# A hybrid transformer trunk on one NeuronCore: forget-gate bias as extra rows of a matmul, and one ring of six weight pieces

## The reference, cut to what matters

```
h = rms_norm(x); u = h @ w_in            # 1024 -> 5384 columns
y_pool = pool_mixer(u[pool])             # trailing windows 2, 4, 8, 16
y_conv = conv_module(u[conv])            # GLU, depthwise conv of 31 taps, LayerNorm, swish
y_attn = forgetting_attention(q, k, v, f_logit)
x = x + (sum of gate_i * (y_i @ w_br_i)) @ w_out
```

## Time and profile before

| | |
|---|---|
| median of 3 runs | 1668.14 us (1666.18 to 1669.09) |
| the profiled execution | 1673.39 us |
| its span, first to last instruction | 1671.5 us |
| mean granted TensorE clock in it | 0.989 of full speed |
| busy share of the span | PE 98%, DVE 77%, ACT 63%, POOL 4% |
| HBM read | 450.74 MB |

### The profile page before, as it was taken

How to read it: one execution, slowest core, us unless ns; L and a number is a source line. 1 busy time by engine, 2 the same in 40 slices (tenths; PEclk the granted TensorE clock), 3 DMA queues, 4 the chain that set the end, 5 groups by cost and what they waited for, 6 DMA issues and landing times.

```text
span 1671.5 us, 25101 instructions
## 1 busy us (share of the span) xinstructions
PE 1634.1 (98%) x9644; PEld 1433.8 (86%) x9644; DVE 1290.0 (77%) x1097; ACT 1056.3 (63%) x908; POOL 61.9 (4%) x60
## 2 busy tenths in 40 slices
PE   7999989999899998999999999999999999999998
PEld 7998989999898897888888888888888888888887
DVE  5973764444697476897997998997988987987986
ACT  5444444454554454677777777777777777777775
POOL 0121100000012110000000000000000000000000
PEclk9999999999999998999999999999999999999999
DMA  9543455556454343799999999999999999999993
GB/s 335 167 146 106 127 167 171 191 175 200 126 170 133 103 133 120 258 377 369 327 374 354 344 371 340 358 372 334 365 371 333 363 375 334 359 377 334 359 377 132
DMA packets 231294, 452.48 MB, mean 271 GB/s; under 512 B 6992, under 2 KB 80720, under 8 KB 231120
## 3 DMA queue, kind: packets, MB, share of 16 engines
q1 hardware_dynamic: 231248, 451.82, 76.7%
HBM read 450.74 MB, written 1.05 MB: 270 GB/s over the span
## 4 chain that ended last, share of the span: by engine, by line
PE 93%; DVE 4%; ACT 2%; issue 1%; DMA 0%; ACTq 0%; DVEq 0%
PE bank L278 28%; PE bank L280 27%; PE bank L279 27%; PE bank L1292 2%; PE bank L1308 1%; DVE w_low L268 1%; PE bank L1326 1%; ACT w_high L264 1%; PE bank L1041 1%; PE bank L1129 1%; DVE h_full L628 1%; DVE rinv L618 0%; PE bank L1131 0%; PE bank L1148 0%; PE bank L1092 0%
## 5 line engine op out<-in xcount | busy, mean ns | idle before, releaser
L268 DVE TENSOR_TENSOR w_low<-raw,w_high 128x2048 fp32r<-128x2048 f32 x427 | 977.8, 2291 | 284.4 <-ACT w_high L264 283.2
L264 ACT ACTIVATE w_high<-raw 128x2048 fp32r<-128x2048 f32 x427 | 818.9, 1919 | 378.1 <-PE bank L280 376.7
L278 PE MATMUL bank<-w_high,hg_high 128*128 128x512 f32 x896 | 354.5, 396 | 0.7 <-issue 0.7
L280 PE MATMUL bank<-w_high,hg_low 128*128 128x512 f32 x896 | 350.1, 391 | 0.0
L279 PE MATMUL bank<-w_low,hg_high 128*128 128x512 f32 x896 | 349.3, 390 | 0.0
L278 PE MATMUL bank<-h_high,w_high 128*128 128x256 f32 x1056 | 301.8, 286 | 6.4 <-DVE h_low L623 4.8
L280 PE MATMUL bank<-h_high,w_low 128*128 128x256 f32 x1056 | 295.3, 280 | 0.0
L279 PE MATMUL bank<-h_low,w_high 128*128 128x256 f32 x1056 | 295.3, 280 | 0.0
L278 PEld LDWEIGHTS bank<-h_high,w_high 128*128 128x128 f32 x1056 | 200.8, 190 | 11.8 <-issue 9.4
L279 PEld LDWEIGHTS bank<-h_low,w_high 128*128 128x128 f32 x1056 | 199.1, 189 | 1.6 <-issue 1.4
L280 PEld LDWEIGHTS bank<-w_high,hg_low 128*128 128x128 f32 x896 | 168.6, 188 | 36.0
(11 more groups left out here) (242 smaller groups left out, 1586.6 us busy)
## 6 DMA issues: line engine op xcount, KB each, us to landing
raw<-exp_w SPq DMA_DIRECT2D x336, 1024.0 KB, 5.3
raw<-w_in SPq DMA_DIRECT2D x42, 1024.0 KB, 5.1
raw<-ffn_w SPq DMA_DIRECT2D x33, 1024.0 KB, 5.3
raw<-w_out SPq DMA_DIRECT2D x8, 1024.0 KB, 4.9
raw<-w_br_attn SPq DMA_DIRECT2D x4, 1024.0 KB, 5.0
raw<-w_br_pool SPq DMA_DIRECT2D x2, 1024.0 KB, 5.2
raw<-w_br_conv SPq DMA_DIRECT2D x2, 1024.0 KB, 4.9
cst<-consts SPq DMA_DIRECT2D x1, 1280.0 KB, 13.4
```

The lines of the kernel that those rows point to most:

```text
L264: nc.scalar.activation(wh[c % SPLIT][:], raw[c % RAW][:], ACT.Copy).then_inc(s["high_done"], 1)
L268: nc.vector.tensor_tensor(wl[c % SPLIT][:], raw[c % RAW][:], wh[c % SPLIT][:].bitcast(F32), ALU.subtract).then_inc(s["split_done"], 1)
L278: pe.matmul(dst, lh, rh, start=start and i == 0, stop=False)
L280: last = pe.matmul(dst, ll, rh, start=False, stop=stop and i == len(terms) - 1)
```

## The change

**Ring.** `raw`, `wh` and `wl` are six buffers each. `raw` and `wl` share their memory: the low half of a piece is written over the loaded piece. So the load of piece c now waits until PE has used piece c-6 (not until its low half is made), and `split_high` waits only for the load, no longer for PE.

**Bias rows.** GpSimd no longer makes `decay`. DVE writes the negated `lf` of the 8 heads twice into a zeroed tile `nlf` (columns 0 to 7 and 32 to 39). After piece 8 PE forms its running sums with three float32 matmuls into bank 6 (`bias_sums`): 64 rows x 384 columns. ACT rounds them to fp32r rows `crow` (step 11), DVE replaces the rows of the second copy by what the rounding lost (step 11). `head_scores` starts with one fp32r matmul over all 384 columns whose weights pick head h's two rows (`sel8`, one column read 128 times), then adds the mask in fp32r twice, then q.k. The rest of the `c_i` term is left to the softmax, where it drops out.

**Order of VectorE.** `head_norm(h)` stands in step 14+h, behind `head_max(h)`; a few taps (`TAPS_AHEAD`) stand between, and `TAPS_AT` is less for steps 12 to 15. The sum stays 62.

The core of the diff:

```diff
-TAPS_AT = {..., 10: 8, 11: 8, 12: 8, 13: 8, 14: 7, 15: 7}
+TAPS_AT = {..., 10: 8, 11: 8, 12: 6, 13: 5, 14: 5, 15: 4}
+TAPS_AHEAD = {12: 2, 13: 3, 14: 2, 15: 3}
...
-        raw = [sb(f"raw{i}", [P, PIECE]) for i in range(RAW)]
-        wh = [sb(f"w_high{i}", [P, PIECE], F32R) for i in range(SPLIT)]
-        wl = [sb(f"w_low{i}", [P, PIECE], F32R) for i in range(SPLIT)]
+        with ExitStack() as loaded:
+            raw = [loaded.enter_context(nc.sbuf_tensor(f"raw{i}", [P, PIECE], F32)) for i in range(RING)]
+        wl = [sb(f"w_low{i}", [P, PIECE], F32R) for i in range(RING)]
+        wh = [sb(f"w_high{i}", [P, PIECE], F32R) for i in range(RING)]
...
         def load_piece(sp, c, r, src, k):
-            if not (isinstance(r, int) and c < RAW):
-                sp.wait_ge(s["split_done"], num(c - RAW + 1, r))
+            if not (isinstance(r, int) and c < RING):
+                sp.wait_ge(s["used"], num(c - RING + 1, r))
...
         def split_high(act, c, r=0):
-            if not (isinstance(r, int) and c < SPLIT):
-                act.wait_ge(s["used"], num(c - SPLIT + 1, r))
...
# GpSimd
-                for h in range(HEADS):
-                    if h >= 2:
-                        pool.wait_ge(s["scores"], 8 * l + h - 1)
-                    for k, (m, tile) in enumerate(((C_UPTO, 0), (C_UPTO, 1), (C_ONES, 0))):
-                        nc.gpsimd.tensor_scalar(decay[:, h % 2, k, :], C(m), lf[:, tile, h:h + 1], None,
-                                                ALU.mult).then_inc(s["decays"], 1)
+                pool.wait_ge(s["f_soft"], 2 * l + 2)
+                nc.gpsimd.memset(nlf[:], 0.0).then_inc(s["nlf_zero"], 1)
+                pool.wait_ge(s["nlf_zero"], l + 1)
+                nc.gpsimd.memset(crow[64:P, :].bitcast(F32), 0.0).then_inc(s["rows_zero"], 1)
...
# ScalarE
+                    if n == 5:
+                        nc.scalar.activation(identr[:], ident, ACT.Copy).then_inc(s["consts_r"], 1)
+                        nc.scalar.activation(maskr[:], C(C_MASK), ACT.Copy).then_inc(s["consts_r"], 1)
+                    if n == 11:
+                        act.wait_ge(s["bias_sum"], l + 1)
+                        nc.scalar.activation(crow[0:64, :], bank[6][0:64, 0:384], ACT.Copy).then_inc(s["bias_high"], 1)
...
# VectorE
-                    if 15 <= n <= 22:
-                        head_norm(n - 15)
                     if 14 <= n <= 21:
                         head_max(n - 14)
+                    run_taps(TAPS_AHEAD.get(n, 0))
...
+                    if 14 <= n <= 21:
+                        head_norm(n - 14)
...
+                    if n == 11:
+                        dve.wait_ge(s["bias_high"], l + 1)
+                        nc.vector.tensor_tensor(crow[32:64, :], bank[6][32:64, 0:384], crow[32:64, :].bitcast(F32),
+                                                ALU.subtract).then_inc(s["bias_low"], 1)
...
# TensorE
+                def bias_sums():
+                    pe.wait_ge(s["nlf_in"], 2 * l + 2)
+                    pe.wait_ge(s["qk_root"], 4 * l + 3)
+                    pe.matmul(bank[6][0:64, 0:128], nlf[:, 0, :], C(C_UPTO), start=True, stop=True)
+                    pe.matmul(bank[6][0:64, 128:384], nlf[:, 0, :], C(C_UPTO, 2), start=True, stop=False)
+                    pe.matmul(bank[6][0:64, 256:384], nlf[:, 1, :], C(C_UPTO), start=False,
+                              stop=True).then_inc(s["bias_sum"], 1)
...
-                    pe.matmul(B[:, 0:128], q[:, 0:P], k[:, 0:P], start=True, stop=False)
-                    pe.matmul(B[:, 0:128], decay[:, h % 2, 0, :], C(C_AFTER), start=False, stop=False)
-                    pe.matmul(B[:, 0:128], ident, C(C_MASK), start=False, stop=True)
-                    pe.matmul(B[:, 128:384], q[:, P:S], k, start=True, stop=False)
-                    pe.matmul(B[:, 128:256], decay[:, h % 2, 2, :], C(C_AFTER), start=False, stop=False)
-                    pe.matmul(B[:, 128:384], decay[:, h % 2, 1, :], C(C_ONES, 2), start=False, stop=False)
-                    pe.matmul(B[:, 256:384], ident, C(C_MASK), start=False, stop=True).then_inc(s["scores"], 1)
+                    pe.matmul(B[:, 0:384], sel8[:, h:h + 1].to_broadcast([P, P]), crow[:], start=True, stop=False)
+                    pe.matmul(B[:, 0:128], identr[:], maskr[:], start=False, stop=False)
+                    pe.matmul(B[:, 256:384], identr[:], maskr[:], start=False, stop=False)
+                    pe.matmul(B[:, 0:128], q[:, 0:P], k[:, 0:P], start=False, stop=False)
+                    pe.matmul(B[:, 128:384], q[:, P:S], k, start=False, stop=True).then_inc(s["scores"], 1)
```

More of the change, by code:

```diff
@@ L49 @@
 NEG = -1e30
-RAW = 6
-SPLIT = 3
+RING = 6
 PIECE = 2048
@@ L159, in trunk @@
             vt = mb("vt", [P, TT, 512])
-            decay = mb("decay", [P, 2, 3, P])
+            crow = mb("bias_rows", [P, 3 * P], F32R)
+            maskr = mb("mask_r", [P, P], F32R)
+            identr = mb("ident_r", [P, P], F32R)
+            nlf = mb("neg_log_forget", [P, TT, 64])
+            sel8 = mb("head_rows", [P, 8], F32R)
             prob = mb("prob", [P, 2, 384])
@@ L209, in trunk @@
             squares norm_stats norm_root norm_h h_high_done h_low_done norm_step
-            f_logits f_soft decay_in decays unit_part ln_taps unit_used_act unit_used_dve
+            f_logits f_soft nlf_zero rows_zero nlf_in consts_r head_rows bias_sum bias_high bias_low unit_part ln_taps unit_used_act unit_used_dve
             qk_sq qk_stats qk_root pool_in_ready pooled_ready pool_lin
@@ L220, in trunk @@
         x_in = [sem(f"x_in{m}") for m in range(4)]
-        raw_in = [sem(f"raw_in{i}") for i in range(RAW)]
+        raw_in = [sem(f"raw_in{i}") for i in range(RING)]
         def C(i, n=1):
@@ L235, in num @@
         def num(c, r):
-            return c if isinstance(r, int) and r == 0 else r * RAW + c
+            return c if isinstance(r, int) and r == 0 else r * RING + c
         def unit_ready(eng, l, u):
@@ L272, in take_piece @@
             pe.wait_ge(s["split_done"], num(c + 1, r))
-            return fold(wh[c % SPLIT][:], k), fold(wl[c % SPLIT][:], k)
+            return fold(wh[c % RING][:], k), fold(wl[c % RING][:], k)
         def products(pe, dst, terms, start=True, stop=True):
@@ L560, in job @@
                     if not isinstance(j, int):
-                        for k in range(SPLIT):
+                        for k in range(3):
                             split_high(act, c + k, r0)
@@ L573, in job @@
                         t_high(r + 1)
-                        silu(r * RAW + (MOE0 + 6))
+                        silu(r * RING + (MOE0 + 6))
                         split_high(act, c + 9, r)
@@ L807, in mixer @@
                         dve.wait_ge(s["act_step"], 2 * l + 2)
-                        nc.vector.tensor_tensor(fg[:, 5, :], fg[:, 4, :], fg[:, 3, :],
-                                                ALU.subtract).then_inc(s["decay_in"], 1)
+                        dve.wait_ge(s["nlf_zero"], l + 1)
+                        for at in (0, 32):
+                            nc.vector.tensor_tensor(nlf[:, :, at:at + 8], fg[:, 3, :].rearrange("p (t h) -> p t h", t=TT),
+                                                    fg[:, 4, :].rearrange("p (t h) -> p t h", t=TT),
+                                                    ALU.subtract).then_inc(s["nlf_in"], 1)
+                        nc.vector.tensor_tensor(sel8[:], ident[:, 0:8], ident[:, 32:40],
+                                                ALU.add).then_inc(s["head_rows"], 1)
+                    if n == 11:
+                        dve.wait_ge(s["bias_high"], l + 1)
+                        nc.vector.tensor_tensor(crow[32:64, :], bank[6][32:64, 0:384], crow[32:64, :].bitcast(F32),
+                                                ALU.subtract).then_inc(s["bias_low"], 1)
                     run_taps(TAPS_AT.get(n, 0))
@@ L976, in job @@
                     r0, c = j * EXP_BLOCKS, MOE0
-                    for k in range(SPLIT if isinstance(j, int) else 0, 4):
+                    for k in range(3 if isinstance(j, int) else 0, 4):
                         split_low(dve, c + k, r0)
@@ L996, in middle @@
                         split_low(dve, c + 9, r)
-                        mult(r + 2, r * RAW + (MOE0 + 8))
+                        mult(r + 2, r * RING + (MOE0 + 8))
                         split_low(dve, c + 10, r)
@@ L1116, in ln_sum @@
                     ins.then_inc(s[name], 1)
-                def head_scores(h):
-                    pe.wait_ge(s["decays"], 3 * (8 * l + h) + 3)
+                def bias_sums():
[5 more added lines that the diff above has]
+                              stop=True).then_inc(s["bias_sum"], 1)
+                def head_scores(h):
+                    if h == 0:
+                        pe.wait_ge(s["bias_low"], l + 1)
+                        pe.wait_ge(s["consts_r"], 2 * l + 2)
+                        pe.wait_ge(s["head_rows"], l + 1)
```

(3 more changed lines are left out.)

12 lines of the change are left out of this document (5 added, 7 removed).

## The result

The changed kernel takes 1642.77 us (median of 4 runs, 1642.18 to 1649.69), the kernel before 1667.99 us (1666.18 to 1669.09). The ratio is 0.986, with a 95% interval of 0.9845 to 0.9874: 25.2 us faster, where 18.9 were forecast and the range of 1637 to 1661 holds the time. The ratios are formed from fast executions alone; two slow ones of the kernel before (2315.08 and 2743.64 us, at a mean granted clock of 0.659 and 0.554) are left out of them.

A forecast was written before the change was run, and what follows sets the result against it. PE was taken to bound the kernel, with 93% of the chain of waits. The terms -18.4 + 2.4 + 0 - 2.9 + 0 gave -18.9 us, from 1673.4 to 1654.5 and, at the median, 1649 us; range 1637 to 1661.

The forecast's parts named there:

- The scores: Attention on PE: each head's scores fall from 2.77 to 1.62 us, 18.4 us gained over 16 heads; bounds 13.6 to 20.8.
- The bias sums: After piece 8 on PE: three added float32 matmuls cost 1.2 us a layer, 2.4 us for both; bounds 1.6 and 3.0.
- The order of VectorE: Attention on DVE: `head_norm(h)` one step earlier and the moved taps cost zero.
- half of the gain is lost: Rival: DVE or ACT late in the faster attention, or late expert pieces; PE saves 9 us net, 1659 us; chance 0.12.
- PE stands three pieces behind DVE there: Attention, step 14: the argument given against the rival that DVE's work there loses half of the gain.
- PE needs the result two pieces later (over 14 us): Attention: the reason given that `head_norm` one step earlier, with DVE waiting for ACT's exponentials, costs zero.
- The ring: Last part of each mixer: idle times of 0.92 and 0.51 us go, 2.9 us for both layers; bounds 0 and 4.0.
- which the change doesn't touch: Last part of a mixer: of PE's 7.2 us idle, the rest beyond 0.92 and 0.51 us is the normalisation, unchanged.
- The expert jobs: Expert jobs: later loads from the ring cost nothing, jobs still 123.6 us; bounds 0 and 17 us.
- 4.1 us of reserve: Expert jobs: 16.3 us from load issue to end of use, 12.2 needed, 4.1 left for queueing on ACT and DVE.
- The pace: Rival: another start shifts the dense stage to PE's faster pace, winning 7 to 8 us more, 1640 us; chance 0.13.
- the offset of 5.3 us to the median: The profiled execution, 1673.4 us, lay 5.3 us above the runs' median of 1668.1, lowering the forecast from 1654.5 to 1649.2.

The follow-up runs named there:

- qk_apart: The changed kernel with the first q.k product moved up between the bias matmul and the masks, same five matmul lines: 1648.27 us, ratio 0.9888.
- order_only: The kernel before with only VectorE's new order (`TAPS_AT`, `TAPS_AHEAD`, place of `head_norm`): 1667.53 us, ratio 1.0005.
- order_undone: The changed kernel with VectorE's old order, the division one step later and all taps after the split: 1649.42 us, ratio 0.99.
- bias_only: The kernel before with the bias rows and new scores alone, old buffers and old order of VectorE: 1656.98 us, ratio 0.9944.
- before_again: The kernel before, unchanged, run once more for a second profile: 1667.67 us.
- ring_only: The kernel before with the ring of six buffers alone; scores, GpSimd's products and VectorE's order as before: 1663.57 us, ratio 0.9977.
- lead4: The changed kernel with each load waiting until PE has used piece c-4 instead of c-6, two buffers less: 1767.57 us, ratio 1.0592.

## Why the prediction was right, and what it left out

*Time.* Forecast 1649, measured 1642.8, in the range and on the forecast's side. Of the terms:

*The scores, -18.4 forecast, -22.8 measured.* The mechanism was right. The term that was mis-sized is the cost of a head after the change, 1.62 forecast and 1.40 measured: both q.k lines were taken at their old steps of 0.41 + 0.63, and they take 0.32 + 0.52 once they follow each other; the masks take 0.27 instead of 0.32. That two of four changes of weight shape go was in the text, but the sum used the old lines; `qk_apart` prices the order of the lines at 0.40 us a head, 6.6 us in all. 16 x 1.37 = 21.9 us. Where transposes follow the scores the stretch shrinks by 1.41 us instead of 1.37 (4.31 to 2.90 us with transposes and values), which makes 22.5 for all heads; the last 0.3 us are pace of the products in mixer 2.

*The bias sums, +2.4 forecast, +2.4 measured.* The rows give 1.0 us a layer, 0.2 less than forecast; the other 0.4 us are pace of the products in mixer 2, so part of the agreement is luck.

*The order of VectorE, 0 forecast.* The text asked what the order costs and found nothing. It didn't ask what the other edits would be worth without it. `order_only` shows 0 and `order_undone` shows 7 us: the order is the cover for the short scores. The text's rival "half of the gain is lost" had the right mechanism, DVE late in the attention, and `bias_only` and `order_undone` are that rival, at the steps 13 and 14 where DVE has its taps; the changed kernel escapes it by its order. Two reasons given were wrong. "PE stands three pieces behind DVE there" holds for the splits, not for the division, which stands behind them. And "PE needs the result two pieces later (over 14 us)" is far too much: even with the new order head 1's division ends at 107.4 us and its transposes start at 113.49, 6.1 us later.

*The ring, -2.9 forecast, -4.7 measured,* beyond the bound of 4.0. The bracketed idle times count from the modelled end of the last matmul: from start to start the two waits cost 1.07 and 0.67 us more than a plain step, not 0.92 and 0.51. And two short waits were left out, 0.26 us for unit 24's bank (183.58 us) and 0.45 us for ACT's squares (0.30 us of idle time at 214.88 us, shown above). That makes 2.4 us a mixer. Against the second profile of the kernel before (`before_again`, 49.75 and 49.57 us) the ends win 4.2 us instead of 4.7. The text had put the rest of the idle time down to the normalisation, "which the change doesn't touch"; the second short wait stands there, and went. The place and mechanism were otherwise right: `ring_only`.

*The expert jobs, 0 forecast, 0 measured.* 123.6 us a job in both, and the estimate of 4.1 us of reserve was about 3.5 by `lead4`.

*The pace, held as a rival worth 7 us.* Its size was right, but it isn't an effect of the change; it is drawn per execution. It took part in the forecast all the same: the sum was made against a profile that had drawn the slow step, and only the offset of 5.3 us to the median, which the text carried along unexplained, brought it from 1654.5 to 1649.2. That the forecast ended 6 us from the result and not 12 is luck.

## What to carry to other kernels

When one engine bounds a stage, shorten its stream, and then look at each in-order engine that feeds it for the instruction that now comes too late: here the short scores won 13 us of PE's time alone, 15.6 with the ring beside them and 23 with the new order of VectorE as well. An edit that is worth nothing alone may be what lets another pay, so undo it in the changed kernel before it is called free. Keep matmuls of one weight shape together; and size a ring by its round trip over the pace of use, with some room for queueing (here 0.7 us on 12.1 in the mean, 1.5 at most).

## What the runs showed that was not expected

- A long stream of fp32r matmuls of 256 columns runs at one of two steps, 113 or 118 ns, in different executions of one kernel, at the same granted clock: 6.8 us of this kernel. Two profiles have to be compared piece by piece before their spans are.
- Two fp32r matmuls of 128 columns step at 0.06 us when they follow one of 384 columns, and at 0.11 us in a row of their own kind.
- A change between 128-row and 64-row weights costs 0.15 to 0.2 us.
- After a wait of 2.3 us in the middle of a busy stretch the granted clock fell in mixer 2 of `order_undone` (mean 0.65 over 4 us, piece 14 longer by 4.1 us) and not in its mixer 1 (1.00, longer by 2.4 us); in `bias_only` it fell after such a wait in both mixers (mean 0.79 over 8 us). What decides is open.
- The two stretches at the changes of stage vary by about 1 us between profiles (14.8 to 16.0 us to the first dense piece in kernels whose instructions there are the same). The routing, from the last piece of mixer 2 to the first expert piece, takes 28.3 to 33.7 us in the 14 profiles.
